# A two-block transformer layer stack on one core: second weight unit of each chunk taken half by half, with new instruction lists

## What is computed

```
for i in range(DEPTH):                         # first block
    h = rms_norm(x, ln_attn_g[i])
    dq, dk, dv, mq, mk, mv = jnp.split(h @ w_in[i], cuts, axis=-1)
    ...                                        # heads normalised; differential and block attention with relative bias
    x = x + jnp.concatenate([y_diff, y_moba], axis=-1) @ w_out[i]
    x = x + conv_ffn(rms_norm(x, ln_ffn_g[i]), w_up[i], conv_w[i], conv_b[i], w_down[i])
for l in range(DEPTH):                         # second block
    x = x + 0.5 * swiglu(rms_norm_2(x, ffn1_norm[l]), ffn1_w_gate[l], ffn1_w_up[l], ffn1_w_down[l])
    proj = rms_norm_2(x, mix_norm[l]) @ w_in[l] + b_in[l]
    ...                                        # forgetting attention; causal conv and gated linear recurrence
    merged = jax.nn.sigmoid(g_attn) * y_attn + jax.nn.sigmoid(g_rnn) * y_rnn
    x = x + merged @ w_out[l]
    x = x + 0.5 * swiglu(rms_norm_2(x, ffn2_norm[l]), ffn2_w_gate[l], ffn2_w_up[l], ffn2_w_down[l])
```

## Time and profile before

| | |
|---|---|
| profiled execution, its own time | 1899.35 us |
| its span from first to last instruction | 1897.6 us |
| median of the runs | 1899.11 us |
| TensorE (PE) busy | 1868.7 us, 98% of the span |
| VectorE (DVE) busy | 1213.9 us, 64% |
| ScalarE (ACT) busy | 1091.0 us, 57% |
| GpSimd (POOL) busy | 43.0 us, 2% |
| HBM read | 338.24 MB, 179 GB/s over the span |
| mean granted TensorE clock | 0.999 |

### The profile page before, as it was taken

The page is one execution under the profiler, slowest core; times in us unless marked ns, Lnnn a source line. Parts: engine busy times, 40 slices in busy tenths (PEclk is TensorE's granted clock), DMA queues, the critical chain, the costliest instruction groups (busy, mean ns, idle before and its releaser), DMA issues.

```text
span 1897.6 us, 24666 instructions
## 1 busy us (share of the span) xinstructions
PE 1868.7 (98%) x9700; PEld 1584.9 (84%) x9700; DVE 1213.9 (64%) x1789; ACT 1091.0 (57%) x1570; POOL 43.0 (2%) x63
## 2 busy tenths in 40 slices
PE   8999999999999999999999999999999999999999
PEld 6879998878999788888888888888888888888887
DVE  6867778686777645557866654555455687565444
ACT  6866556776555543459865544354435887545442
POOL 2000000000000000000010100000000002000000
PEclk9999999999999999999999999999999999999999
DMA  8444555455565455544554655554554546454553
GB/s 273 140 133 170 187 195 183 156 158 174 180 199 179 163 193 199 200 148 164 193 196 157 229 171 198 189 188 172 184 198 157 178 155 212 163 207 162 178 200 111
DMA packets 157773, 340.92 MB, mean 180 GB/s; under 512 B 6182, under 2 KB 19083, under 8 KB 157147
## 3 DMA queue, kind: packets, MB, share of 16 engines
q1 hardware_dynamic: 154400, 327.24, 50.3%
q0 software_dynamic: 2800, 11.91, 2.1%
q10 hardware_dynamic: 459, 0.20, 0.0%
HBM read 338.24 MB, written 1.09 MB: 179 GB/s over the span
## 4 chain that ended last, share of the span: by engine, by line
PE 88%; ACT 5%; DVE 5%; issue 1%; DMA 1%; ACTq 0%; DVEq 0%
PE bank L472 28%; PE bank L474 27%; PE bank L473 27%; DVE w_lo L2020 2%; PE bank L556 1%; ACT w_hi L1272 1%; ACT tmp L1531 1%; PE bank L782 1%; PE bank L521 1%; PE bank L870 1%; DVE tmp L2690 1%; PE bank L805 1%; PE bank L826 0%; DMA tmp<-in_conv_w 0%; PE bank L1039 0%
## 5 line engine op out<-in xcount | busy, mean ns | idle before, releaser
L2020 DVE TENSOR_TENSOR w_lo<-raw,w_hi 128x1024 fp32r<-128x1024 f32 x620 | 734.3, 1221 | 159.4 <-ACT w_hi L1272 151.7
L1272 ACT ACTIVATE w_hi<-raw 128x1024 fp32r<-128x1024 f32 x620 | 635.4, 1054 | 318.4 <-PE bank L474 246.9
L472 PE MATMUL bank<-w_hi,r_hi 128*128 128x512 f32 x1344 | 534.9, 398 | 5.4 <-DVE r_lo L2044 3.6
L474 PE MATMUL bank<-w_hi,r_lo 128*128 128x512 f32 x1344 | 525.0, 391 | 0.0
L473 PE MATMUL bank<-w_lo,r_hi 128*128 128x512 f32 x1344 | 524.1, 390 | 0.0
L472 PEld LDWEIGHTS bank<-w_hi,r_hi 128*128 128x128 f32 x1344 | 253.0, 188 | 60.2 <-issue 5.7
L474 PEld LDWEIGHTS bank<-w_hi,r_lo 128*128 128x128 f32 x1344 | 252.7, 188 | 54.1
L473 PEld LDWEIGHTS bank<-w_lo,r_hi 128*128 128x128 f32 x1344 | 253.3, 188 | 49.8
L472 PE MATMUL bank<-w_hi,z_hi 128*128 128x512 f32 x656 | 259.1, 395 | 0.0
L474 PE MATMUL bank<-w_hi,z_lo 128*128 128x512 f32 x656 | 255.9, 390 | 0.0
L473 PE MATMUL bank<-w_lo,z_hi 128*128 128x512 f32 x656 | 255.5, 389 | 0.0
(11 more groups left out here) (219 smaller groups left out, 1598.7 us busy)
## 6 DMA issues: line engine op xcount, KB each, us to landing
raw<-in_w_in SPq DMA_DIRECT2D x79, 1024.0 KB, 5.1
raw<-in_ffn_w_down SPq DMA_DIRECT2D x44, 1024.0 KB, 5.0
raw<-in_w_up SPq DMA_DIRECT2D x40, 1024.0 KB, 5.2
raw<-in_ffn_w_gate SPq DMA_DIRECT2D x40, 1024.0 KB, 5.2
raw<-in_ffn_w_up SPq DMA_DIRECT2D x40, 1024.0 KB, 5.4
raw<-in_w_down SPq DMA_DIRECT2D x22, 1024.0 KB, 4.9
raw<-in_w_out SPq DMA_DIRECT2D x16, 1024.0 KB, 5.0
raw<-in_w_o_rnn SPq DMA_DIRECT2D x8, 1024.0 KB, 5.7
```

Of the source, the lines that this page charges most:

```text
L472: pe.matmul(out_, lh, rh, start=start, stop=False, skip_group_check=True)
L474: return pe.matmul(out_, ll, rh, start=False, stop=stop, skip_group_check=True)
L1272: A_(w_hi[:, n % NH, :], raw[:, u % NS, HALF * h:HALF * (h + 1)], ACT.Copy).then_inc(hi_ready, 1)
L2020: return V.tensor_tensor(dst, src, hi.bitcast(F32), ALU.subtract)
```

## The change

In `quarter`, the second unit is now used as the first one is: call n takes half n of the unit for token tile 0 and then for token tile 1. Each call waits for its own half of `w_lo`; before, call 0 waited for both. `half_done` is given when token tile 0 is complete, in call 1 after its first six matmuls; `part_done` is given at the end of each call.

```
-                elif n == 0:
-                    pe.wait_ge(lo_ready, 2 * u + 2)
-                    for kk in range(4):
-                        mm = tile(0, kk)
-                    mm.then_inc(half_done, 1)
                 else:
-                    for kk in range(4):
-                        mm = tile(1, kk)
-                        if kk % 2:
-                            mm.then_inc(part_done, 1)
+                    pe.wait_ge(lo_ready, 2 * u + n + 1)
+                    for t in range(TB):
+                        tile(t, 2 * n)
+                        mm = tile(t, 2 * n + 1)
+                        if t == 0 and n:
+                            mm.then_inc(half_done, 1)
+                    mm.then_inc(part_done, 1)
```

The lists of TensorE, ScalarE and VectorE are written anew for the start, the first block's attention stage and the second block's mix stage; in the feed-forward networks two calls move. No instruction is added or removed by the lists. The core of it:

```
-                turn_gains()
                 x_first(0)
                 x_first(1)
                 x_first(2)
                 x_first(3)
+                turn_gains()
                 turn_params(0)
-                turn_params(1)
                 part(0, 0)
...
                 part(4, 3)
-                part(5, 0)
-                part(5, 1)
                 turn(where, 2)
                 scores(where, 4)
+                part(5, 0)
                 turn(where, 3)
+                part(5, 1)
                 part(5, 2)
...
                 part(6, 1)
-                turned(4)
                 part(6, 2)
                 part(6, 3)
-                lru_linear(3)
+                turned(4)
```

VectorE in the feed-forward network of the second block:

```
+                    lo(uj + 2, 0)
                     product(j, 0)
-                    lo(uj + 2, 0)
                     product(j, 1)
```

More of the change, by code:

```diff
@@ L1214, in _ @@
                 gate_part(1, 3)
+                weigh(where, 1)
                 gated_part(1, 0)
-                weigh(where, 1)
                 gated_part(1, 1)
@@ L1682, in _ @@
                 stage_chunk(2, 1)
+                hi(u0 + 7, 0)
+                hi(u0 + 7, 1)
+                squares_of(2)
                 hi(u0 + 8, 0)
-                squares_of(2)
                 hi(u0 + 8, 1)
                 hi(u0 + 9, 0)
+                hi(u0 + 9, 1)
                 deviations(2)
-                hi(u0 + 9, 1)
                 exps(where, 0)
+                hi(u0 + 10, 0)
+                exps(where, 1)
                 store(2, 0)
+                copy_turned(where, 0)
                 store(2, 1)
-                exps(where, 1)
                 stage_chunk(3, 0)
@@ L1695, in _ @@
                 squares_of(3)
-                copy_turned(where, 0)
-                hi(u0 + 10, 0)
+                deviations(3)
                 hi(u0 + 10, 1)
-                deviations(3)
-                hi(u0 + 11, 0)
                 exps(where, 2)
@@ L1704, in _ @@
                 copy_turned(where, 1)
+                exps(where, 3)
+                hi(u0 + 11, 0)
                 hi(u0 + 11, 1)
                 hi(u0 + 12, 0)
+                copy_turned(where, 2)
+                copy_turned(where, 3)
                 hi(u0 + 12, 1)
-                exps(where, 3)
-                copy_turned(where, 2)
+                exps(where, 4)
                 hi(u0 + 13, 0)
-                copy_turned(where, 3)
-                exps(where, 4)
                 stage_diff(1)
@@ L1972, in _ @@
                 hi(u + 29, 0)
+                att_high(where, 2)
                 hi(u + 29, 1)
-                att_high(where, 2)
+                sigmoid(1, 1)
                 hi(u + 30, 0)
+                copy_turned(where, 3)
                 hi(u + 30, 1)
-                copy_turned(where, 3)
+                att_high(where, 3)
                 hi(u + 31, 0)
-                sigmoid(1, 1)
-                att_high(where, 3)
                 hi(u + 31, 1)
+                sigmoid(2, 0)
@@ L2889, in _ @@
+                normalise(where, 1)
                 logits(where, 2)
-                lo(u + 24, 0)
-                lo(u + 24, 1)
-                normalise(where, 1)
                 normalise(where, 2)
-                att_low(where, 0)
-                lo(u + 25, 0)
                 lo(u + 25, 1)
                 lo(u + 26, 0)
+                att_low(where, 0)
+                logits(where, 3)
                 lo(u + 26, 1)
+                gated(0, 0)
+                gated(0, 1)
                 lo(u + 27, 0)
-                logits(where, 3)
@@ L2901, in _ @@
-                gated(0, 0)
+                lo(u + 27, 1)
+                att_low(where, 1)
                 gate(1, 0)
-                lo(u + 27, 1)
-                gated(0, 1)
-                att_low(where, 1)
                 gate(1, 1)
                 lo(u + 28, 0)
+                att_low(where, 2)
+                normalise(where, 3)
                 lo(u + 28, 1)
-                normalise(where, 3)
                 lo(u + 29, 0)
                 lo(u + 29, 1)
-                att_low(where, 2)
```

360 lines of the change are left out of this document (180 added, 180 removed).

## The result

The changed kernel takes 1908.89 us (median of 5 runs, 1908.27 to 1910.28), the kernel before 1899.07 us (1897.65 to 1899.61): ratio 1.0053, interval [1.0042, 1.0063]. It is slower by 9.8 us. The forecast was 1893.0, a gain.

A forecast was written before the change was run, and what follows sets the result against it. TensorE, busy 1868.7 of 1897.6 us, was taken as the bound, so only its gaps could shrink. Terms 1.2 + 1.4 + 0.6 + 0.5 + 0.8 + 1.9 = 6.4 us off 1899.35 gave 1893.0; range 1889.5 to 1897.0.

The forecast's parts named there:

- Start: Kernel start: reordered transposes and weight halves let the first product begin at 10.8 us, 1.2 us earlier (bounds 0.6, 1.6).
- Attention of block 1: First block's attention, both layers: shorter PE gaps and a steadier clock, gains of 1.4, 0.6, 0.5 and 0.8 us.
- (a): Block 1 attention: PE's 0.69 us wait for normalise(3), ahead of turn(3), closes in both layers, gaining 1.4 us.
- (b): Block 1 attention: PE's 1.10 us wait for copy_turned(5) shrinks by 0.3 us, gaining 0.6 us for both layers.
- (c): Block 1 attention: PE's 1.1 us wait for att_low(7) shrinks by 0.25 us, gaining 0.5 us for both layers.
- (d): Block 1 attention: the half-speed clock window from 105.1 us costs 1.7 us; half counted as gained, 0.8 us.
- Mix stage: Mix stages: PE's waits of 1.47 and 0.25 us for w_lo at part(6, 2) close, gaining 1.9 us with restarts.
- The range: Whole kernel: 1889.5 to 1897.0 us, the lower end from all upper bounds together, a gain of 9.2 us.
- rival (2): Late token tiles stop PE at gate_part(1, 0); from 0.10 us a chunk, 10 us against 6.4, slower by 3.8; chance 0.04.
- What is later, at nothing: Second units: half_done comes 1.4 us later in all 100 chunks, priced at no cost because VectorE stands idle there.
- rival (1): Some 200 moved list places open new PE gaps of 0.5 to 1 us, giving back 3 us: 1896 to 1899; chance 0.20.
- The clock by bank alternation: Rival: bank changes in each call open small gaps and clock drops, 1.7 us each; six give 1903 us; chance 0.02.

The follow-up runs named there:

- e4: Changed kernel with sigmoid(3, 1) of the mix stages put back in ScalarE's list, behind merged_high(0, 0): 1902.29 us, ratio 1.0019.
- e5: Changed kernel with GpSimd's load for the next layer held until layer 0's mix stage has added its last sum to x: 1900.88 us, ratio 1.0012.
- e8: Changed kernel with three mix-list rows put back: store(7, 1), sigmoid(3, 1) and the two add_out(0, t): 1899.13 us, ratio 1.0005.
- e9: Changed kernel with the three rows of e8 put back and four more rows moved in the mix stages and block 1: 1900.72 us, ratio 1.0007.
- e11: Kernel before, all its lists; second unit starts token tile 0 on the first w_lo half, waits for the second before its third k tile: 1898.75 us, ratio 1.0000.
- e14: e7 with two more moves: forget_sums behind part(8, 3), block 1's add_out(0, 0) and add_out(0, 1) ahead of lo(u0 + 17, 0): 1897.36 us, ratio 0.9994.
- e1: Kernel before with only the new half-by-half second half of quarter, all lists as before: 1919.29 us, ratio 1.0108.
- e10: e1 with one row of the plain feed-forward loop moved, lo(uj + 2, 0) ahead of product(j, 0): 1907.76 us, ratio 1.0050.
- e3: Changed kernel with add_out(0, 0) and add_out(0, 1) of the mix stages put back ahead of lo(u + 41, 0) and lo(u + 41, 1): 1905.22 us, ratio 1.0039.
- e6: Changed kernel with store(7, 1) of the mix stages put back ahead of hi(u + 24, 0) in ScalarE's list: 1906.14 us, ratio 1.0041.
- e7: Changed kernel with the mix-stage lists of PE, ScalarE and VectorE as before; new quarter and other new lists stay: 1897.74 us, ratio 0.9994.
- e12: Lists of e9, with the split-wait quarter of e11 in place of the half-by-half order: 1899.37 us, ratio 1.0001.
- e13: e10 with a second row moved, block 1's copy_v(5, 0) behind logits(where, 5): 1901.32 us, ratio 1.0020.
- e15: e14 with the split-wait quarter of e11 in place of the half-by-half order: 1896.61 us, ratio 0.9988.

## Why the prediction was wrong

**Start, 1.2 us:** right. The first product starts at 10.94 instead of 12.05 us, against a forecast of 10.8.

**Attention of block 1, 3.3 us:** right on the places, too large in size. (a) The two gaps of `turn(3)`, 0.7 us each, closed. (b), (c) The waits before `weigh(5)` and for `att_low(7)` fell by 0.13 us each, not by 0.3 and 0.25: the chain through `turn(5)` and `att_high(7)` binds more than I gave it. New gaps of 1.1 us at 65.8 (`store(2, 0)`, now behind `exps(1)`) and of 0.3 and 0.7 behind the late `add_out` took back as much as all of this. At 818.3 us the change was 1.6 ahead, where the terms up to there promised 4.5. And most of these 1.6 us are term (d). At 99 us the change is 0.1 us ahead (99.21 against 99.31); behind the window of the earlier trace rows it is 1.9 ahead, rows of the kernel before and of the changed one:

```profile
122.80 0.50 PE L472 MATMUL bank<-w_hi,y_hi 128*128 128x512 f32 x1 [1.08 <-DVE y_lo L2020]
```
```profile
120.88 0.50 PE L472 MATMUL bank<-w_hi,y_hi 128*128 128x512 f32 x1 [0.95 <-DVE y_lo L2016]
```

**(d) the clock, 0.8 us:** in this pair of profiles all of the 1.7 us was gained, since the window is in the one and not in the other; whether it comes is in part chance. The low window at 106 us is in the profiles of the kernel before and of the runs e4, e5, e8, e9, e11 and e14 (in e1 and e10 it starts at about 102), and not in those of the changed kernel, e3, e6, e7, e12, e13 and e15. Windows of two runs whose lists there are the same, with three moves and with the mix lists of before:

```profile
106.00:108.30 2.30, 2.30 (x9) 1.72 (x6) 1.32 (x6) 2.30 (x7) 0.00 (x0) 0.50 0.00 0
```
```profile
106.00:108.30 2.30, 2.30 (x15) 1.92 (x14) 2.18 (x13) 2.30 (x4) 0.00 (x0) 1.00 0.00 0
```

The mean clock that every run lists shows how often such things happen: it is below 1.000 in 19 of 27 runs of the kernel before (those beside e15) and in 8 of 11 of e11, which has its lists. With the new lists of block 1 it is so in 1 of 11 (e7) to 8 of 11 (e9) under the half-by-half order, and in none of the 22 runs of e12 and e15, which have the split wait. So how often the clock falls depends on the order too. The two groups of runs of the kernel before lie 1.9 us apart (1897.1 and 1899.0), as much as most of these versions differ from it. The number of half-speed matmuls at the start, 5 (e7) to 12 (e4), adds to the spread.

**Mix stage, 1.9 us:** the wait closed as I said, and gave little. In the changed kernel `w_lo` waits of 0.40 and 0.43 us came at another place; in e7 and e11 `forget_sums` took it up.

**The range:** the upper bounds, 9.2 us, lead to 1890.2 and not to 1889.5, and 10 us against 6.4 in rival (2) is slower by 3.6 and not 3.8. Neither matters here, as the time fell 11.9 us above the range.

**Two steps failed.** The first, for the order, is "*What is later, at nothing*": "`half_done` comes ... 1.4 us later, in all 100 chunks", with the earlier trace rows as its cover. Two errors are in it. The delay is 1.4 us only where the two calls are neighbours; in block 1 a list of other work stands between them, and it was 5 us (e10). And I asked who reads token tile 0, found VectorE idle, and so free of charge. But an idle VectorE is one that stands at a wait, with its list behind it: its 11.08 us of idle time became 12.49, and the `w_lo` behind it came 0.9 us too late for PE, 12 times (e1, e10). My rival (2) had the sign and the semaphore, with the wrong victim. Under the old lists it costs 20 us. The new lists hold both rows of e10 and e13, so the changed kernel pays little of it: 0.3 us or more of added waiting for `r_lo` at each of four norms. I had read these rows as repairs of gaps.

**The second step, which made the changed kernel slow,** is the silence on the last part of the mix lists. I followed the lists "only around known gaps" and priced the rest, rival (1), at 3 us by what a misplaced row had cost so far, 0.5 to 1 us. With these lists as before the time is 11.2 us less (e7). The end of layer 0's mix stage cost most of it (8.0 by e5, against 2.8 for the two gaps of e6), because three things met: a sigmoid computed late, which moved GpSimd's load onto the request for the second gate unit; a transfer of 13.3 us for that unit; and sums queued behind it. Behind the stop came the low clock, which the prediction had priced only at other places. e4 and e5 each undo most of it.

**The clock by bank alternation:** did not happen. The clock was at 1.00 through the second units, which change banks every 6 matmuls, and at its lower level only at the start and behind stops of PE. The Trainium skill, TensorE: Matmul & The Clock Gate, section "A second HAM failure mode: psum-queue depth-cycling", describes such an order with small idle times between groups of matmuls; here the matmuls of a unit follow each other at 0.23 us without them.

**Still open:** 2.5 us of the half-by-half order's cost (e13 against before). The waits in e13's profile name candidates that no run tested: 0.3 to 0.5 us more at each of four norms, 0.7 us more ahead of `turn_diff` in each layer of block 1 (1.56 against 0.85), and 1.4 us at `forget_sums`, against 1.7 us of `w_lo` waits that are gone. Open is also what makes the clock fall at 106 us in one run and not in the next.

## What to carry to other kernels

When a semaphore comes later, ask not who reads it, but what stands behind its reader in that engine's list; the engine's idle time at that wait is no cover for it. Where a signal moves into the next call, its delay is everything that the list has between the two calls. Starting early on a first half can be had without moving the signal, at no cost (e11, 1.0000); that it gains something by itself no run shows. A list written for one order can be 10 us and more off for another, so the two are to be judged only together. Before you move a row whose result releases a large load, look at who else asks for DMA in these few us. And when versions differ by 2 us or less, compare runs that list the same mean clock before you credit a list with the difference.

## What the hardware showed that I had not expected

A load of 1 MB took 13.34 us when another engine's load of 1.5 MB was issued 0.3 us ahead of it, against a median of 5.2; from 1067 to 1073 us the DMA share was 1.00, so all 16 engines were busy. With the same load issued 4.6 us ahead it took 7.7. A stop of PE of 3.7 us costs twice: in the changed kernel the stretch behind it, from the norm at 1078.9 to that at 1270.7, took 4.0 us more than before, 3.3 of them by the low clock.

And the same VectorE instructions of `lru_scan(3)` in layer 1 took 0.68 and 1.27 us in e5 (where the next one took 1.58 instead of 0.69), and 1.1 and 1.0 us more in the changed kernel, of which these are the rows:

```profile
1593.12 1.78 DVE L2702 TENSOR_TENSOR tmp<-tmp 128x512 f32<-128x512 f32 x1
1594.94 2.23 DVE L2705 TENSOR_TENSOR_SCAN tmp<-tmp 128x256 f32<-128x256 f32 x2
```

I do not know what lengthens them. They stand on the way to `logits(0)` and `exps(0)`, and PE's gap there is 1.8 us in the one and 0.65 in the other; e5's layer 0, with the long times, has the long gap too. With the row of e6 back, the gap is short beside long scans as well (e6 and e8, layer 1), so the scans alone don't make it.
